# Another order for a routing stage and for the last units of an expert turn

## The chip, the core and the metric

The kernel runs on one core of a Trainium2 chip. TensorE (PE) multiplies matrices, VectorE (DVE) and ScalarE (ACT) work on tiles, GpSimd (POOL) and SyncE (SP) mostly issue transfers here. Each engine works through its own list of instructions in order and waits on semaphores for the others. The metric is the device time of one launch in microseconds (us).

## The reference, cut to what is computed

One step of a two-layer encoder over 256 prompt and 64 sample tokens (T = 320) of width 1024, all float32. Layer 0 is a pooling mixer and a dense SwiGLU, layer 1 is attention and then the part that matters here, eight experts of which each token takes two:

```
def _moe(h, w_router, b_router, w1, w3, w2):
    logits = jnp.einsum('btd,de->bte', h, w_router, ...) + b_router.astype(jnp.float32)
    vals, idx = lax.top_k(logits, TOP_K)
    gates = jax.nn.softmax(vals, axis=-1)
    gate_full = jnp.sum(jax.nn.one_hot(idx, N_EXPERTS, ...) * gates[..., None], axis=-2)
    y = jnp.zeros_like(h)
    for e in range(N_EXPERTS):
        y = y + gate_full[..., e:e + 1].astype(h.dtype) * _swiglu(h, w1[e], w3[e], w2[e])
    return y
...
        e_ple = p[i].astype(x.dtype) @ w_ple_proj[i]
        gate = jax.nn.sigmoid(_rmsnorm(x, g_ple[i]) @ w_ple_gate[i])
        x = x + gate * e_ple
```

The inner width of an expert is 3584.

## The kernel before

**Precision by three products.** Each operand is split in a high and a low part (`Sh`, `Sl` for weights, `Ah`, `Al` for activations), and a product is three matmuls: high by high, high by low, low by high. All matmuls of this kind pass the helper at line 609.

**Weights as units.** Weights come in units of 128 x 2048 numbers, 1 MB each. SP loads a unit into one of six slots of `raw` (line 207), ACT writes its high part into one of three slots of `Sh` in two halves (`hi`, line 365), DVE writes the low part into `Sl` in two halves (`lo`, line 961). SP may load unit q once the low part of unit q - 6 is done (line 206). ACT starts on unit q when PE is done with unit q - 3.

**Routing stage.** After the attention's output and a norm, PE multiplies by the router's weights, ACT adds the bias (line 555), PE transposes the logits (line 834). DVE takes the two largest of each token (lines 1172 to 1180), marks them in `sel` (line 1190), and builds the gates from an exponential that ACT computes (line 558). PE sums `sel` to give each token its place within its expert (`pos_done`), DVE turns this to `posm`, counts whether an expert has more than 128 tokens (lines 1204 to 1208, semaphore `routed`), builds one-hot rows for expert 0 (`one_hots`, line 1214), and PE makes from them the list of token numbers (`slot_info`), which DVE writes to `ix` (line 1226). Meanwhile the 320 token rows have to get to DRAM: PE transposes them in six blocks (`rows(0)` to `rows(5)`, line 827), ACT copies each block out of PSUM to `hrow` (line 564), SP stores three pieces to `rows_dram` (line 252). When all are stored, POOL issues an indirect DMA that gathers the 128 rows of expert 0 into `xrow` (line 341). PE transposes these (`gather`, line 851), ACT and DVE split them (lines 569 and 966), and the first expert unit can start. Before PE starts the loop, and before SP loads any unit beyond the first six of expert 0, each reads the count (`routed`).

**Expert turns.** A loop of m * 8 + 8 turns follows; here m is 0, so there are eight. A turn has 42 units n = 0 to 41: for each of seven blocks two units `g`, two units `u`, and behind the next block's two units `d`. The last eight units are g6 (34, 35), u6 (36, 37), d5 (38, 39) and d6 (40, 41). For each block, ACT takes the silu of g (line 587), DVE multiplies it with u (line 1264, semaphore `gum_ready`), PE transposes the product (`transposes`, line 900), ACT and DVE split it (`high_t`, line 581; `low_t`, line 966), and the two `d` units of that block multiply it. In the last units PE also transposes the next expert's rows (`gather(i + 2)`, line 851), which ACT and DVE split (`high_x`, `low_x`).

The order is written out by hand: each engine has its own program, with the actions of unit n ahead of its `hi(n + 3)` or `lo(n + 3)`. In the last units it is: before unit 38 the gather's transposes, between 38 and 39 `transposes(6)`, and d6 (unit 40) waits for `low_t(6)`. The lines that the change touches are 253, 557 to 564, 590 to 594, 824 to 845, 919 to 926, 1204 to 1232 and 1271 to 1275.

## Time and profile before

| | |
|---|---|
| median of 3 runs | 1625.07 us (1623.9 to 1625.52) |
| the profiled execution | 1625.96 us, of which the span from the first to the last instruction is 1623.9 us |
| mean granted TensorE clock | 0.977 of full speed |
| busy, share of the span | PE 1535.5 us (95%), DVE 1227.1 us (76%), ACT 1010.6 us (62%), POOL 43.9 us (3%) |
| routing stage | about 538 to 571 us of the span |
| the eight expert turns | about 571 to 1557 us, 123.3 us each |

The profile gives times in us from the span's start. A busy PE is no PE at its peak, since matmuls are pipelined: what counts is the step from one start to the next. In the turns the step of a matmul with 512 columns is 0.23 us.

### The profile page before, as it was taken

The numbers are of one execution on the slowest core, as the hardware profiler recorded it, in microseconds if no ns is written. First come the engines' busy times: TensorE is split into PE (matmuls) and PEld (weight loads), VectorE is DVE, ScalarE is ACT, GpSimd is POOL, SyncE is SP. The second block draws the span as 40 slices with busy tenths as digits, with TensorE's granted clock in tenths as the row PEclk, the third lists the DMA queues.
The fourth block names the chain that finished last, engine by engine and source line by source line (L and its number), as shares of the span: only waits on it lengthen the run. The fifth ranks groups of instructions, "written<-read, shape, count | busy, mean of one in ns | idle before, by whom it ended". The sixth has DMA issues, their size and how long they took to land.

```text
span 1623.9 us, 23510 instructions
## 1 busy us (share of the span) xinstructions
PE 1535.5 (95%) x8088; PEld 1333.8 (82%) x8088; DVE 1227.1 (76%) x1484; ACT 1010.6 (62%) x1289; POOL 43.9 (3%) x45
## 2 busy tenths in 40 slices
PE   2799999999899599999999999999999999999987
PEld 1699999999889388888878878878878888888877
DVE  6643434446754479999999999999899899899884
ACT  2433333345554367777777777777777777777763
POOL 6000000000000000000000000000000000000000
PEclk7999999999999789999999999999999999999999
DMA  7154444443320369989999989989989989999930
GB/s 277 30 175 140 151 155 155 140 154 130 116 86 27 120 229 373 379 333 375 370 339 374 379 331 372 384 334 369 379 333 373 381 338 363 375 340 357 383 121 33
DMA packets 64552, 429.33 MB, mean 264 GB/s; under 512 B 8208, under 2 KB 11920, under 8 KB 13440
## 3 DMA queue, kind: packets, MB, share of 16 engines
q1 hardware_dynamic: 61232, 423.24, 68.8%
q0 software_dynamic: 1392, 4.90, 0.9%
q10 hardware_dynamic: 1888, 0.64, 0.2%
q8 instruction: 26, 0.43, 0.1%
q14 instruction: 14, 0.11, 0.0%
HBM read 425.49 MB, written 3.27 MB: 264 GB/s over the span
## 4 chain that ended last, share of the span: by engine, by line
PE 86%; DVE 8%; issue 3%; ACT 2%; DMA 1%; SPq 0%; DVEq 0%; ACTq 0%; POOLq 0%
PE PS L609 84%; DVE s_Sl L961 2%; DVE s_Al L966 2%; PE PS L900 1%; DVE s_rstd L970 1%; ACT s_Sh L365 1%; DVE s_hT L983 1%; DMA s_G<-rows_dram,s_ix 1%; DMA s_raw<-in_w_trunk 1%; DVE s_G L1007 1%; PE PS L780 0%; DVE s_hT L1029 0%; DVE s_G L1022 0%; DVE s_hT L1027 0%; ACT s_std L382 0%
## 5 line engine op out<-in xcount | busy, mean ns | idle before, releaser
L961 DVE TENSOR_TENSOR s_Sl<-s_raw,s_Sh 128x1024 fp32r<-128x1024 f32 x790 | 929.9, 1220 | 205.9 <-ACT s_Sh L365 201.4
L365 ACT ACTIVATE s_Sh<-s_raw 128x1024 fp32r<-128x1024 f32 x798 | 800.2, 1053 | 272.6 <-PE PS L609 269.2
L609 PE MATMUL PS<-s_Sh,s_Ah 128*128 128x512 f32 x1344 | 531.9, 396 | 10.0 <-DVE s_Al L966 10.0
L609 PE MATMUL PS<-s_Sh,s_Al 128*128 128x512 f32 x1344 | 525.3, 391 | 0.0
L609 PE MATMUL PS<-s_Sl,s_Ah 128*128 128x512 f32 x1344 | 525.3, 391 | 0.0
L609 PE MATMUL PS<-s_Ah,s_Sh 128*128 128x320 f32 x1008 | 317.7, 315 | 41.1 <-DVE s_Al L966 39.9
L609 PE MATMUL PS<-s_Al,s_Sh 128*128 128x320 f32 x1008 | 315.0, 313 | 0.0
L609 PE MATMUL PS<-s_Ah,s_Sl 128*128 128x320 f32 x1008 | 315.0, 313 | 0.0
L609 PEld LDWEIGHTS PS<-s_Sh,s_Ah 128*128 128x128 f32 x1344 | 253.3, 188 | 62.5 <-DVE s_Sl L961 12.6
L609 PEld LDWEIGHTS PS<-s_Sh,s_Al 128*128 128x128 f32 x1344 | 253.0, 188 | 54.2
L609 PEld LDWEIGHTS PS<-s_Sl,s_Ah 128*128 128x128 f32 x1344 | 253.4, 189 | 48.5
L609 PEld LDWEIGHTS PS<-s_Ah,s_Sh 128*128 128x128 f32 x1008 | 192.5, 191 | 46.1 <-issue 37.6
L609 PEld LDWEIGHTS PS<-s_Al,s_Sh 128*128 128x128 f32 x1008 | 192.6, 191 | 0.2
L609 PEld LDWEIGHTS PS<-s_Ah,s_Sl 128*128 128x128 f32 x1008 | 192.4, 191 | 0.0
L966 DVE TENSOR_TENSOR s_Al<-PS,s_Ah 128x512 fp32r<-128x512 f32 (+1 forms) x82 | 53.7, 663 | 17.1 <-ACT s_Ah L569 11.5
L587 ACT ACTIVATE s_G<-PS 128x512 f32<-128x512 f32 x56 | 33.5, 599 | 43.1 <-PE PS L609 43.1
L388 ACT ACTIVATE s_Ah<-s_hT 128x320 fp32r<-128x320 f32 x48 | 22.1, 469 | 53.9 <-DVE s_hT L1029 27.4
L412 ACT ACTIVATE s_sq<-PS 128x320 f32<-128x320 f32 x28 | 10.7, 434 | 67.0 <-PE PS L609 67.0
L966 DVE TENSOR_TENSOR s_Al<-s_G,s_Ah 128x640 fp32r<-128x640 f32 x14 | 11.5, 825 | 41.5 <-ACT s_Ah L416 41.5
L416 ACT ACTIVATE s_Ah<-s_G 128x640 fp32r (+1 forms) x14 | 10.2, 736 | 52.3 <-PE PS L609 46.9
L1053 DVE TENSOR_TENSOR s_G<-s_sq,PS 128x320 f32 (+1 forms) x28 | 12.4, 484 | 39.5 <-PE PS L609 39.5
L609 PE MATMUL PS<-s_sq,s_ones 128*128 128x320 f32 x112 | 33.9, 459 | 7.5 <-POOL s_lg L308 5.9
(156 smaller groups left out, 771.4 us busy)
## 6 DMA issues: line engine op xcount, KB each, us to landing
s_raw<-in_w_moe SPq DMA_DIRECT2D x336, 1024.0 KB, 4.9
s_raw<-in_w_trunk SPq DMA_DIRECT2D x63, 1024.0 KB, 4.9
s_xT<-in_xT SPq DMA_DIRECT2D x2, 640.0 KB, 5.4
out_yT<-s_hT SPq DMA_DIRECT2D x4, 320.0 KB, 2.4
rows_dram<-s_G SPq DMA_DIRECT2D x2, 512.0 KB, 2.8
s_pT<-in_pT ACTq DMA_DIRECT2D x1, 320.0 KB, 24.2
s_pT<-in_pT SPq DMA_DIRECT2D x1, 320.0 KB, 3.1
rows_dram<-s_G SPq DMA_DIRECT2D x1, 256.0 KB, 3.1
```

The lines of the kernel that those rows point to most:

```text
L365: nc.scalar.activation(Sh[:, q % NSPL, o:o + UNIT // 2], raw[:, q % NRAW, o:o + UNIT // 2], ACT.Copy).then_inc(hi_ready, 1)
L388: nc.scalar.activation(Ah3[:, c, :], hT[:, c, :], ACT.Copy).then_inc(hh_ready, 1)
L412: nc.scalar.activation(sg[:, f, :], PS[:, f, 0:T], ACT.Silu).then_inc(silu_done, 1)
L587: nc.scalar.activation(sgm[:, b % 2, :], PS[:, 2 + 2 * (b % 2), :], ACT.Silu).then_inc(msilu_done, 1)
L609: return nc.tensor.matmul(out, w, m, start=start, stop=stop, **kw)
L900: last = nc.tensor.transpose(PS[:, 0, P * q:P * q + P], gum[:, b % 2, P * q:P * q + P], ident[:, :])
L961: last = nc.vector.tensor_tensor(Sl[:, q % NSPL, o:o + UNIT // 2], raw[:, q % NRAW, o:o + UNIT // 2], Sh[:, q % NSPL, o:o + UNIT // 2].bit ...
L966: return nc.vector.tensor_tensor(out, x, high.bitcast(F32), ALU.subtract).then_inc(done, 1)
L970: link(nc.vector.reciprocal(rstd[:, :], std[:, :]))
L983: nc.vector.scalar_tensor_tensor(out=hT[:, c, :], in0=xT[:, c, :], scalar=vec[:, g, c:c + 1], in1=rstd[:, :], op0=ALU.mult, op1=ALU.mult). ...
L1007: nc.vector.scalar_tensor_tensor(out=hcat[:, c, o:o + b - a], in0=xT[:, c, a:b], scalar=vec[:, G_MIX0, c:c + 1], in1=rstd[:, a:b], op0=ALU ...
L1053: nc.vector.tensor_tensor(out(f), sg[:, f, :], PS[:, 2 + f, 0:T], ALU.mult).then_inc(gu_ready, 1)
```

## The change

Nothing is computed in another way; instructions stand in another order, and one wait is added.

- ACT copies the row blocks 0, 1 and 2 ahead of the exponential of the gates and 3, 4 and 5 behind it, and loads the silu table behind all six. Before, all six stood behind the exponential and the table load.
- PE transposes all five remaining row blocks ahead of the sums over `sel`. Each block has a PSUM bank of its own (2 + n, before 2 + n % 4), so that blocks 4 and 5 wait for no copy.
- DVE builds the one-hot rows of expert 0 first and counts for `routed` afterwards.
- SP waits for the gathered rows (`xrow_loaded`) before it reads the count and goes on loading units 6, 7 and so on of expert 0.
- In the last units of a turn, `transposes(6)` with `high_t(6)` and `low_t(6)` stand directly behind the gather's transposes, ahead of unit 38 and ahead of `high_x` and `low_x`; before, they stood behind unit 38.

```diff
                 sp.dma_start(rows_dram[P * t:P * t + r, :], hrow[0:r, t, :]).then_inc(rows_stored, 16)
+            sp.wait_ge(xrow_loaded, 16)
             sp.wait_ge(routed, 1)
...
-            act.wait_ge(top_ready, 1)
-            nc.scalar.activation(rt[:, :, 1], rt[:, :, 0], ACT.Exp).then_inc(gexp_ready, 1)
-            table(ACT.Silu)
             for n in range(6):
+                if n == 3:
+                    act.wait_ge(top_ready, 1)
+                    nc.scalar.activation(rt[:, :, 1], rt[:, :, 0], ACT.Exp).then_inc(gexp_ready, 1)
                 act.wait_ge(hrow_done, n + 1)
                 t, half = n // 2, n % 2
                 r = TS if t == 2 else P
-                nc.scalar.activation(hrow[0:r, t, 512 * half:512 * half + 512], PS[0:r, 2 + n % 4, :], ACT.Copy).then_inc(hrow_ready, 1)
+                nc.scalar.activation(hrow[0:r, t, 512 * half:512 * half + 512], PS[0:r, 2 + n, :], ACT.Copy).then_inc(hrow_ready, 1)
+            table(ACT.Silu)
...
                     if n == NU - 4:
+                        high_t(NBK - 1)
                         high_x(0, i * 2 + 3)
                         high_x(1, i * 2 + 4)
-                    if n == NU - 3:
-                        high_t(NBK - 1)
...
-                if n >= 4:
-                    pe.wait_ge(hrow_ready, n - 3)
                 for q in range(4):
-                    last = nc.tensor.transpose(PS[0:r, 2 + n % 4, P * q:P * q + P], hT[:, 4 * half + q, P * t:P * t + r], ident[:, :])
+                    last = nc.tensor.transpose(PS[0:r, 2 + n, P * q:P * q + P], hT[:, 4 * half + q, P * t:P * t + r], ident[:, :])
...
-            rows(1)
-            rows(2)
+            for n in range(1, 6):
+                rows(n)
             pe.wait_ge(sel_ready, 1)
...
             last.then_inc(pos_done, 1)
-            for n in range(3, 6):
-                rows(n)
...
                         gather(i + 2)
+                        transposes(NBK - 1)
...
-                        if POS[kind, b] + h == NU - 3:
-                            transposes(NBK - 1)
...
             one_hots(0, 1)
+            link(most)
+            nc.vector.tensor_scalar(cnt[0:1, 1:2], cnt[0:1, 0:1], float(P), None, ALU.is_gt)
...
+            nc.vector.tensor_copy(extra[0:1, 0:1], cnt[0:1, 3:4]).then_inc(routed, 1)
             take_slots(1)
...
                     if n == NU - 4:
+                        low_t(NBK - 1)
                         low_x(0, i * 2 + 3)
                         low_x(1, i * 2 + 4)
-                    if n == NU - 3:
-                        low_t(NBK - 1)
```

How the instructions then stand, engine by engine (no time is in these rows; the changed kernel's line numbers differ by a few). First place, ACT in the routing stage: `s_G` is the tile that holds `hrow`, the 3-column `s_rt` is the exponential. Before:

```order
L555 ACTIVATE s_lgT<-PS,s_br 8x320 [waits lgT_done,small_loaded]
L558 ACTIVATE s_rt<-s_rt 128x3 [waits top_ready]
L372 ACT_TABLE_LOAD
L372 ACTIVATE s_spare<-s_eps 128x1
L564 ACTIVATE s_G<-PS 128x512 [waits hrow_done] x4
L564 ACTIVATE s_G<-PS 64x512 [waits hrow_done] x2
```

And now:

```order
L556 ACTIVATE s_lgT<-PS,s_br 8x320 [waits lgT_done,small_loaded]
L565 ACTIVATE s_G<-PS 128x512 [waits hrow_done] x3
L561 ACTIVATE s_rt<-s_rt 128x3 [waits top_ready]
L565 ACTIVATE s_G<-PS 128x512 [waits hrow_done]
L565 ACTIVATE s_G<-PS 64x512 [waits hrow_done] x2
L373 ACT_TABLE_LOAD
L373 ACTIVATE s_spare<-s_eps 128x1
```

Three copies moved ahead of the exponential, and the table load behind all six. Second place, SP between the row stores and the first load of the loop. Before:

```order
L252 DMA rows_dram<-s_G 128x1024 [waits hrow_ready] x2
L252 DMA rows_dram<-s_G 64x1024 [waits hrow_ready]
L254 TENSOR_LOAD s_extra [waits routed]
L254 ISA x2
L255 UNCONDITIONAL_BRANCH
L255 ISA
L207 ISA [waits lo_ready]
L207 DMA s_raw<-in_w_moe 128x2048
```

And now:

```order
L252 DMA rows_dram<-s_G 128x1024 [waits hrow_ready] x2
L252 DMA rows_dram<-s_G 64x1024 [waits hrow_ready]
L255 TENSOR_LOAD s_extra [waits routed,xrow_loaded]
L255 ISA x2
L256 UNCONDITIONAL_BRANCH
L256 ISA
L207 ISA [waits lo_ready]
L207 DMA s_raw<-in_w_moe 128x2048
```

The read of the count, and with it every later load, now also waits for the gathered rows. Third place, the last units of a turn, PE from the gather's transposes on. Before:

```order
L851 MATMUL PS<-s_ident,s_G 128x128 [waits xrow_loaded]
L851 MATMUL PS<-s_ident,s_G 128x128 x7
L619 REGISTER_ALU [waits tl_ready]
L609 MATMUL PS<-s_Sh,s_Ah 128x512 [waits lo_ready]
L609 MATMUL PS<-s_Sl,s_Ah 128x512
```

And now:

```order
L848 MATMUL PS<-s_ident,s_G 128x128 [waits xrow_loaded]
L848 MATMUL PS<-s_ident,s_G 128x128 x7
L894 REGISTER_ALU
L897 MATMUL PS<-s_ident,s_G 128x128 [waits tl_ready,gum_ready]
L897 MATMUL PS<-s_ident,s_G 128x128 x3
L620 REGISTER_ALU [waits tl_ready]
L610 MATMUL PS<-s_Sh,s_Ah 128x512 [waits lo_ready]
```

The four transposes of the last product, with their wait for it, stand ahead of unit 38's matmuls. On DVE at the same place (the 128x1024 rows are halves of weight passes, `th_ready` is the product's split, `xh_ready` that of the gathered rows), before:

```order
L961 TENSOR_TENSOR s_Sl<-s_raw,s_Sh 128x1024 [waits hi_ready]
L959 REGISTER_ALU
L961 TENSOR_TENSOR s_Sl<-s_raw,s_Sh 128x1024 [waits hi_ready]
L1220 ISA
L966 TENSOR_TENSOR s_Al<-PS,s_Ah 128x512 [waits xh_ready]
L1220 REGISTER_ALU
L966 TENSOR_TENSOR s_Al<-PS,s_Ah 128x512 [waits xh_ready]
L959 REGISTER_ALU
L961 TENSOR_TENSOR s_Sl<-s_raw,s_Sh 128x1024 [waits hi_ready]
L959 REGISTER_ALU
L961 TENSOR_TENSOR s_Sl<-s_raw,s_Sh 128x1024 [waits hi_ready]
L966 TENSOR_TENSOR s_Al<-PS,s_Ah 128x512 [waits th_ready]
```

And now:

```order
L1261 TENSOR_TENSOR s_G<-s_G,PS 128x512 [waits unit_done]
L955 REGISTER_ALU
L957 TENSOR_TENSOR s_Sl<-s_raw,s_Sh 128x1024 [waits hi_ready]
L955 REGISTER_ALU
L957 TENSOR_TENSOR s_Sl<-s_raw,s_Sh 128x1024 [waits hi_ready]
L962 TENSOR_TENSOR s_Al<-PS,s_Ah 128x512 [waits th_ready]
L1212 ISA
L962 TENSOR_TENSOR s_Al<-PS,s_Ah 128x512 [waits xh_ready]
L1212 REGISTER_ALU
L962 TENSOR_TENSOR s_Al<-PS,s_Ah 128x512 [waits xh_ready]
```

The split of the product moved ahead of the two of the gathered rows and of one weight pass; the product itself (first row, line 1264 before) keeps its place ahead of the weight pass of unit 40.

## Rows read from the trace of the kernel before

**Rows 1.** The page, section 4: what ended last, by engine.
```profile
PE 86%; DVE 8%; issue 3%; ACT 2%; DMA 1%; SPq 0%; DVEq 0%; ACTq 0%; POOLq 0%
```
**Rows 2.** PE's waits, whole span: us in total, times, longest.
```profile
PE PS L851 <- DMA s_G<-rows_dram,s_ix: 12.4, 1, 12.4
```
**Rows 3.** The chain, 540 to 575 us: start, us, what.
```profile
555.38 3.11 DMA rows_dram<-s_G
...
559.39 8.81 DMA s_G<-rows_dram,s_ix
...
568.24 1.13 PE PS L851 x4
...
570.96 4.21 PE PS L609 x9
```
**Rows 4.** Timeline of ACT, 546 to 557: start, us, operation, idle before.
```profile
550.69 0.21 ACT L558 ACTIVATE s_rt<-s_rt 128x3 f32<-128x3 f32 x1 [1.84 <-DVE s_rt L1180]
...
552.32 3.03 ACT L564 ACTIVATE s_G<-PS 128x512 f32<-128x512 f32 x6
```
**Rows 5.** Timeline of PE, 546 to 572 us.
```profile
549.16 1.09 PE L827 MATMUL PS<-s_ident,s_hT 128*128 128x128 f32 x8
551.54 0.18 PE L609 MATMUL PS<-s_sel,s_trib 128*128 128x8 bf16 x1 [1.29 <-DVE s_sel L1190]
```
**Rows 6.** Timeline of DVE, 548 to 572 us.
```profile
551.40 0.16 DVE L1193 TENSOR_SCALAR s_rt<-s_rt 128x3 f32<-128x3 f32 x1
...
552.53 0.18 DVE L1201 SCALAR_TENSOR_TENSOR s_posm<-PS,s_sel 128x24 f32<-128x24 f32 x1
...
555.91 0.15 DVE L1226 CAST s_ix<-PS 128x1 uint32<-128x1 f32 x1
```
**Rows 7.** Timeline of SP's queue, 480 to 640 us.
```profile
553.41 2.43 SPq L252 DMA_DIRECT2D rows_dram<-s_G  x3
558.25 81.12 SPq L207 DMA_DIRECT2D s_raw<-in_w_moe  x24
```
**Rows 8.** Gather, line 341: nine issues, times to landing.
```profile
L341 POOL DMA_INDIRECT s_G<-rows_dram,s_ix x9: 1049/1160/1183, 559.4 to 1515.2; - x9
...
DMA to landing us min/median/max: 5.1/5.6/8.9
```
**Rows 9.** DMA queues, 559.3 to 563.8 us: packets, MB, share of engines.
```profile
q1 hardware_dynamic: 213, 1.61, 91.4%
```
**Rows 10.** The same from 559.3 to 568.3 us.
```profile
q0 software_dynamic: 144, 0.52, 15.6%
```
**Rows 11.** The same from 652.3 to 655.4 us, the second gather.
```profile
q1 hardware_dynamic: 129, 0.97, 75.1%
q0 software_dynamic: 15, 0.06, 4.8%
```
**Rows 12.** The page, section 6: an expert load, KB, us to landing.
```profile
s_raw<-in_w_moe SPq DMA_DIRECT2D x336, 1024.0 KB, 4.9
```
**Rows 13.** Stretches: us, busy share of engines, PEclk, DMA share, GB/s.
```profile
61.65:65.04 3.39, 3.39 (x13) 3.39 (x14) 3.39 (x9) 1.86 (x4) 0.00 (x0) 0.50 0.02 5
...
570.96:577.04 6.08, 6.08 (x14) 4.84 (x15) 1.41 (x3) 1.07 (x2) 0.00 (x0) 0.50 0.00 0
```
**Rows 14.** Timeline of PE, end of turn 2, 806.4 to 815.3.
```profile
806.71 1.03 PE L851 MATMUL PS<-s_ident,s_G 128*128 128x128 f32 x8
807.50 0.47 PE L609 MATMUL PS<-s_Sh,s_Ah 128*128 128x512 f32 x1
...
813.31 0.39 PE L609 MATMUL PS<-s_Sh,s_Al 128*128 128x512 f32 x1
814.86 0.49 PE L609 MATMUL PS<-s_Sh,s_Ah 128*128 128x512 f32 x1 [1.16 <-DVE s_Al L966]
```
**Rows 15.** Timeline of DVE, the same stretch.
```profile
805.45 2.35 DVE L961 TENSOR_TENSOR s_Sl<-s_raw,s_Sh 128x1024 fp32r<-128x1024 f32 x2
807.71 0.68 DVE L1264 TENSOR_TENSOR s_G<-s_G,PS 128x512 f32<-128x512 f32 x1
...
814.05 0.68 DVE L966 TENSOR_TENSOR s_Al<-PS,s_Ah 128x512 fp32r<-128x512 f32 x1
```
**Rows 16.** Waits of all engines, 700 to 1550 us: total, times, longest.
```profile
ACT s_Sh L365 <- PE PS L609: 164.7, 228, 2.2
...
PE PS L609 <- DVE s_Al L966: 7.0, 6, 1.2
```

More of the change, by code:

```diff
@@ L1203, in _ @@
             nc.vector.tensor_scalar(posm[:, :, :], posm[:, :, :], -1.0, None, ALU.add).then_inc(stepped, 1)
-            link(nc.vector.reduce_max(cnt[0:1, 0:1], PS[0:1, 1, 24:32], AX.X))
-            nc.vector.tensor_scalar(cnt[0:1, 1:2], cnt[0:1, 0:1], float(P), None, ALU.is_gt)
-            link(nc.vector.tensor_scalar(cnt[0:1, 2:3], cnt[0:1, 0:1], float(2 * P), None, ALU.is_gt))
-            link(nc.vector.tensor_tensor(cnt[0:1, 3:4], cnt[0:1, 1:2], cnt[0:1, 2:3], ALU.add))
-            nc.vector.tensor_copy(extra[0:1, 0:1], cnt[0:1, 3:4]).then_inc(routed, 1)
+            most = nc.vector.reduce_max(cnt[0:1, 0:1], PS[0:1, 1, 24:32], AX.X)
             def one_hots(e, steps):
@@ L1232, in _ @@
             one_hots(0, 1)
+            link(most)
+            nc.vector.tensor_scalar(cnt[0:1, 1:2], cnt[0:1, 0:1], float(P), None, ALU.is_gt)
+            link(nc.vector.tensor_scalar(cnt[0:1, 2:3], cnt[0:1, 0:1], float(2 * P), None, ALU.is_gt))
+            link(nc.vector.tensor_tensor(cnt[0:1, 3:4], cnt[0:1, 1:2], cnt[0:1, 2:3], ALU.add))
+            nc.vector.tensor_copy(extra[0:1, 0:1], cnt[0:1, 3:4]).then_inc(routed, 1)
             take_slots(1)
```

## The prediction

> **What bounds the kernel.** I read the chain of what ended last, then PE's waits, then the two places that the diff touches, engine by engine in order of time. PE carries 86% of the chain [rows 1], so time can go only where PE stands still or where its work shrinks, and the change shrinks none. Two standstills lie where it works. The large one is a single wait of 12.4 us for the gathered rows of expert 0 [rows 2]. The chain shows what it is made of [rows 3]: the last store of token rows is issued at 555.38 and takes 3.11 us; POOL issues the gather at 559.39, 0.90 us after that landing; the gather takes 8.81 us, to 568.20; and 2.76 us of transposes and splits follow until the first expert matmul at 570.96. The small one comes once a turn: unit 40's first matmul starts 1.55 us after unit 39's last, where the step is 0.23, so 1.32 us are lost to the split of the last product [rows 14, 15]; the waits count it six times for six turns, 1.2 us at most [rows 16], and it is alike in all eight.
>
> **Routing, first half: the stores start earlier.** The six copies run at 0.505 us each, from 552.32 to 555.35, behind the exponential at 550.69 and a table load [rows 4]. The blocks they copy are ready sooner than that. PE did blocks 1 and 2 in 1.09 us from 549.16, 0.55 us a block [rows 5]; with five blocks in a row, block 5 is done at about 551.9 to 552.0. So three copies fit ahead of the exponential, which slips from 550.69 to about 550.9, and the other three run from about 551.1 to 552.6. The last store is then issued near 552.65 and not at 555.38: **2.7 us earlier**. What hides the slips: the exponential's result is first used at 551.40 [rows 6], 0.3 us after it would be there. The sums over `sel` start at 551.54 [rows 5] and move behind block 5, to about 551.95; their 0.4 us end at about 552.4, just before DVE needs them at 552.53 [rows 6]. Without that cover the list of token numbers would be later by what it slips, but that list is ready at 556.06 [rows 6] and POOL's new issue would be at 552.65 + 3.11 + 0.90 = 556.66, so another 0.6 us are free even if DVE's count, now behind the one-hot rows, brought nothing. The table load and the weight pass behind the copies fall into PE's wait and cost nothing. Ends for this term: 2.3 if the copies run into the blocks or the exponential, 3.0 if they don't at all.
>
> **Routing, second half: the gather alone.** Before, SP issues loads from 558.25 on [rows 7], ahead of the gather. In the first 4.4 us after the gather's issue every one of the 213 packets belongs to those loads [rows 9]; then its 144 packets go beside them, 15.6% of 9.0 us or 1.4 us of engine time in all [rows 10]. Now SP waits until the gather has landed, so nothing runs beside it. No row shows a gather alone. From above: the late start may be the gather's own, since it is the kernel's first, and then it takes 4.4 + 1.4 + some 0.4 to finish, 6.2 us. From below: the second gather has its first 15 packets within 3.1 us although loads take 75% of the engines [rows 11]; 2.8 + 1.4 gives 4.2 us. I take 5.6 us, the median of the nine gathers [rows 8]: same instruction, same bytes, and between the two ends. That gives 8.8 - 5.6 = **3.2 us** (2.6 to 4.6).
>
> The Trainium skill (DMA: Bandwidth & Descriptors, Queues, rings and completion order) says that each DMA engine takes turns between the queues that have work for it, packet by packet, which speaks against the wait on SP: loads would slow a gather but not hold it back. The packets after 563.8 agree [rows 10], the empty 4.4 us don't follow from it [rows 9]. By that rule the late start is the gather's own and the term is 8.8 - 6.2 = 2.6 us. The skill (SBUF — State Buffer, Who interferes with whom) also has a DVE instruction with two SBUF inputs hold up a GpSimd instruction that reads SBUF; the gather would now be issued beside DVE's weight pass. The trace shows 1.05 us for the first issue and 1.18 at most with DVE busy [rows 8], a cost of 0.1; by the page one whole DVE half pass, 1.2 us, could be lost, and the sum would be 1618.0.
>
> **What the new wait holds up.** Behind it in SP's queue stand the reading of the count and every load from unit 6 on. The gather now lands at about 556.66 + 5.6 = 562.3. From the end of the last store's issue at 555.84 to the first load SP took 2.4 us [rows 7], with `routed` set long before; so the first load goes at 564.7, lands 4.9 us later [rows 12] at 569.6, and the next two at steps of some 2.6. PE starts expert 0 near 565.0 and the first six units are in place. A unit is twelve matmuls: about 5.1 us at the half clock, then 3.0. ACT wants unit 6 when unit 3 is done, near 579. So the loads have some 9 us to spare, and this wait costs nothing; in the turns before, ACT never waited for a load [rows 16].
>
> **The clock.** PE restarts at the half clock, 0.50, and kept it for 6.08 us from 570.96 on; elsewhere it kept it for 3.39 us after a pause [rows 13]. A matmul's step is 0.425 there against 0.23, so each us of it costs 0.46. It may thus bring up to 1.2 us, or cost some 0.3. I count zero.
>
> **The end of a turn.** Now `transposes(6)` stand right behind the gather's, ahead of unit 38. They need the product, and DVE makes that from 807.71 to 808.39, since the weight pass that began at 805.45 is in front of it [rows 15]; nothing there is moved. PE would be free at 807.50 [rows 14]. A release takes 0.13 us (814.05 + 0.68 to 814.86), so PE stands from 807.50 to 808.52: 1.02 us. What came late is then early: split by ACT at 809.8, by DVE behind its pass at 811.3, and d6 wants it at 814.6. So a wait of 1.32 us is replaced by one of 1.02: 0.30 us a turn, eight turns, **2.4 us**. Queued behind on ACT and DVE are the split of the next rows, not needed before the next turn, and the passes for unit 41, which would be done near 815.3 and are wanted near 817.3. Ends: 0 if the restart behind the transposes costs again what it costs today, 3.6 if DVE is a little earlier.
>
> **The sum.** 2.7 + 3.2 + 2.4 = 8.3 us. Against the profiled execution, 1625.96, that is 1617.7; that run is 0.9 above the median, and from the median, 1625.07, it is **1616.8 us**. All low ends with 0.3 for the clock: 2.3 + 2.6 + 0 - 0.3 = 4.6, so 1620.5. All high ends with 1.2: 3.0 + 4.6 + 3.6 + 1.2 = 12.4, so 1612.7. A measurement of this kernel can tell about 0.2%, 3.25 us, from no change.
>
> **Rivals.**
> - The gather is slow on its own account: without loads it still takes 6.2 to 8.8 us. For it speaks the empty start [rows 9], against it the eight later ones [rows 8]. At 8.8 the term is gone: 1625.07 - 5.1 = 1620.0; at 6.2 it is 1617.4. By the skill's rule on taking turns, above, this is the case. Chance 0.12.
> - All terms near their high ends: about 1613. Chance 0.10.
> - The wait at the turn's end goes altogether, as the order suggests if the product were ready: 8 x 1.32 = 10.6 in place of 2.4, so 1608.5. DVE's rows speak against it [rows 15]. Chance 0.04.
> - The weights come late: PE stops at unit 6 and gives the gain back. It decides from a first load that lands 9 us later than worked out, after 579; some 8 us beyond that is no change, 1625. Against it stand the spare time and the six loaded units. Chance 0.04.
> - **Slower:** PE's new wait for the product is longer than the old one. If DVE came to the product only after the next weight pass, 2.35 us [rows 15], the wait would be 3.4 us in place of 1.32, 8 x 2.05 = 16.4 us, and with 5.9 gained in routing the time 1635.6. It is slower by over 0.2% from a wait of 1.32 + (5.9 + 3.25) / 8 = 2.5 us a turn. The order of DVE's rows speaks against it: the product stays ahead of that pass. Chance 0.04.
>
> **Chances.** The forecast, 1614.5 to 1619, has 0.66. Faster by over 0.2% are the forecast, the slow gather, the high ends and the vanished wait: 0.92; within 0.2% 0.04; slower 0.04. From 1613.0 to 1620.5 lie the forecast, the slow gather and most of the high ends, about 0.86; the others are left out.
>
> **What would show it.** In the changed profile the last row store should be issued near 552.6 and the gather near 556.7; it should land in 4.2 to 6.2 us, and SP's next load should come only after it; the first expert matmul near 565. ACT should show no wait for a load of expert weights. At each turn's end PE's wait for the split of the last product should be gone, and one of about 1.0 us for the product should stand ahead of unit 38. I am wrong if the gather still takes over 8 us, if PE waits at unit 6 for weights, or if the new wait is over 1.3 us.

## The result and the profile after

The changed kernel takes 1615.23 us (median of four runs, 1614.95 to 1615.46) against 1625.30 (1623.9 to 1625.55) measured beside it: a ratio of 0.994 with a 95% interval of 0.9922 to 0.9957, 10.1 us less. The forecast was 1616.8 us with a range of 1613.0 to 1620.5, 8.3 us less. The profiled execution took 1615.06 us, its span 1613.0 us, 10.9 less than the span before.

**Where the time went.** I cut both spans at three points that both traces have: the start of the reciprocal of the norm ahead of the router (539.19 before), the first expert matmul (570.96 before), and the first transpose of the gathered rows in turn 8.

| stretch | before | after | difference |
|---|---|---|---|
| start to the norm's reciprocal | 539.19 | 538.26 | -0.93 |
| reciprocal to the first expert matmul | 31.77 | 24.57 | -7.20 |
| from there to the last transposes of gathered rows | 975.37 | 970.37 | -5.00 |
| from there to the end | 77.58 | 79.81 | +2.23 |

The chain of what ended last, by engine (the page of the changed kernel; answers to [rows 1]):

```profile
PE 89%; DVE 6%; issue 2%; ACT 2%; DMA 1%; SPq 0%; DVEq 0%; ACTq 0%; POOLq 0%
```

The chain of the routing stage, 540 to 575 us of the changed kernel: start, us, what (answers to [rows 3]):

```profile
551.19 3.09 DMA rows_dram<-s_G
...
555.18 4.89 DMA s_G<-rows_dram,s_ix
...
560.11 1.13 PE PS L848 x4
...
562.83 12.30 PE PS L610 x44
```

From the norm's reciprocal on, the last store is issued after 12.93 us and not after 16.19. 0.36 of these 3.26 us lie in the router's matmuls, whose clock differs between the two executions; 2.9 are the change's. The gather takes 4.89 us in place of 8.81, 3.92 less. PE's waits, whole span: us in total, times, longest (answers to [rows 2, 16]):

```profile
PE PS L848 <- DMA s_G<-rows_dram,s_ix: 6.8, 1, 6.8
PE PS L897 <- DVE s_G L1261: 5.7, 8, 0.7
```

The long wait fell from 12.4 to 6.8 us. The second row is the new wait for the product, once in each turn. PE's old wait for the split, `DVE s_Al`, has no row any more between 700 and 1550 us, and ACT and PE have none for a load of expert weights. ACT in the routing stage (timeline; start, us, operation, idle before; answers to [rows 4]):

```profile
547.57 0.60 ACT L565 ACTIVATE s_G<-PS 128x512 f32<-128x512 f32 x1
548.56 1.09 ACT L565 ACTIVATE s_G<-PS 128x512 f32<-128x512 f32 x2 [0.39 <-PE PS L826]
549.53 0.21 ACT L561 ACTIVATE s_rt<-s_rt 128x3 f32<-128x3 f32 x1
549.63 1.54 ACT L565 ACTIVATE s_G<-PS 128x512 f32<-128x512 f32 x3
551.19 1.28 ACT L373 ACT_TABLE_LOAD   x1
```

Three copies stand ahead of the exponential, which starts 0.1 us after its input is there, and the other three follow without a gap. The gathers (line 342; answers to [rows 8]) and the DMA queues from 555.1 to 560.1 us (answers to [rows 9, 10]):

```profile
L342 POOL DMA_INDIRECT s_G<-rows_dram,s_ix x9: 1157/1162/1760, 555.2 to 1502.1; - x9
...
DMA to landing us min/median/max: 4.9/5.8/7.8
```
```profile
q0 software_dynamic: 144, 0.52, 31.7%
```

The gather's 144 packets are alone, since no other queue has a row. By the packets' own times the first comes 2.47 us after the issue; before it was 4.50. POOL's instruction, though, takes 1.76 us, where it took 1.05 before: the maximum in the first row is this gather. SP's queue (answers to [rows 7]):

```profile
549.18 2.47 SPq L252 DMA_DIRECT2D rows_dram<-s_G  x3
561.41 77.90 SPq L207 DMA_DIRECT2D s_raw<-in_w_moe  x27
```

The first load goes 1.34 us after the rows have landed (555.18 + 4.89 = 560.07). Turn 2's end, PE and then DVE (answers to [rows 14, 15]):

```profile
797.41 1.03 PE L848 MATMUL PS<-s_ident,s_G 128*128 128x128 f32 x8
799.16 0.66 PE L897 MATMUL PS<-s_ident,s_G 128*128 128x128 f32 x4 [0.71 <-DVE s_G L1261]
799.57 0.47 PE L610 MATMUL PS<-s_Sh,s_Ah 128*128 128x512 f32 x1
799.88 0.39 PE L610 MATMUL PS<-s_Sl,s_Ah 128*128 128x512 f32 x1
...
804.89 0.39 PE L610 MATMUL PS<-s_Sh,s_Al 128*128 128x512 f32 x1
805.12 0.39 PE L610 MATMUL PS<-s_Sh,s_Ah 128*128 128x512 f32 x1
```
```profile
796.15 2.35 DVE L957 TENSOR_TENSOR s_Sl<-s_raw,s_Sh 128x1024 fp32r<-128x1024 f32 x2
798.42 0.68 DVE L1261 TENSOR_TENSOR s_G<-s_G,PS 128x512 f32<-128x512 f32 x1
799.02 2.35 DVE L957 TENSOR_TENSOR s_Sl<-s_raw,s_Sh 128x1024 fp32r<-128x1024 f32 x2
801.29 1.88 DVE L962 TENSOR_TENSOR s_Al<-PS,s_Ah 128x512 fp32r<-128x512 f32 x3
```

Eight transposes took 0.79 us before (806.71 to 807.50 in [rows 14]), so PE could have gone on at 798.20; the product's transposes start at 799.16, 0.96 us later and 0.06 after the product is done. Counted by steps it is a little less: from the eighth transpose to the ninth it takes 0.98 us, where one transpose follows the other by 0.11, so PE stands 0.87 us. Unit 40 follows unit 39 at 805.12 at the plain step of 0.23. The turn went from 123.27 to 122.63 us: 0.64 less, eight times 5.1.

**The clock.** Of the remaining differences none lies where the change is. Half-clock stretches (PEclk 0.50, the level of 1.2 GHz) fall at other places in the two executions. Ahead of the norm, the one near 410 us lasts 6.83 us in the kernel before and 3.41 in the changed one, which comes to it 0.3 us late and leaves it 0.9 us early. Behind the restart of the experts they got shorter, 6.08 to 4.93 us ([rows 13] and the first row here); behind turn 8 they got longer, which the last row of each kernel shows (columns as in [rows 13]; first the changed kernel, then the kernel before):

```profile
562.83:567.76 4.93, 4.93 (x12) 3.87 (x13) 1.41 (x3) 0.52 (x1) 0.00 (x0) 0.50 0.95 394
...
1554.22:1561.05 6.83, 6.25 (x14) 4.00 (x13) 1.00 (x3) 1.59 (x4) 0.00 (x0) 0.50 0.00 0
```
```profile
1580.56:1583.97 3.41, 3.25 (x12) 2.90 (x12) 3.24 (x8) 3.20 (x9) 0.00 (x0) 0.50 0.00 0
```

What the longer one covers stands in PE's rows: the sixteen sums of squares of the norm behind the last turn, which follow each other by 0.53 us at the half clock and by 0.27 otherwise (timeline; first the changed kernel, then the kernel before):

```profile
1555.78 7.17 PE L610 MATMUL PS<-s_sq,s_ones 128*128 128x320 f32 x16 [0.58 <-DVE s_xT L1242]
```
```profile
1569.18 4.57 PE L609 MATMUL PS<-s_sq,s_ones 128*128 128x320 f32 x16 [0.59 <-DVE s_xT L1245]
```

Of the 14 kernels profiled here, six have 6.83 us of it there: these sums take 6.9 to 7.2 us, and the last stretch lasts 79.0 to 79.8. The other eight have 3.41 us behind these sums or none (but for one at the very end, which all 14 have): the sums take 4.57 us, and the last stretch lasts 76.0 to 77.6, a shorter end of turn 8 included. So some 2.8 us of any kernel here hang on where that stretch falls. In this execution the clock gave -0.93 ahead of the norm, -0.36 at the router, -0.55 behind the restart and +2.87 at the end (the 2.23 of the table and the 0.64 that turn 8 saves there), +1.0 in all. The change itself is worth 2.9 + 3.9 + 5.1 = 11.9 us, of which 10.9 are seen.

### The profile page after: what moved, and what is told of

Same layout as the page of the kernel before. It is cut to its first block, busy times and chain, and to the rows that moved or that the text cites. A ratio compares the mean times of both kernels' runs of the same rounds, so it can differ in the third digit from the quotient of the medians.

```text
span 1613.0 us, 23511 instructions
## 1 busy us (share of the span) xinstructions
PE 1535.2 (95%) x8088; PEld 1334.2 (83%) x8088; DVE 1227.6 (76%) x1484; ACT 1012.1 (63%) x1289; POOL 44.6 (3%) x45
## 4 chain that ended last, share of the span: by engine, by line
PE 89%; DVE 6%; issue 2%; ACT 2%; DMA 1%; SPq 0%; DVEq 0%; ACTq 0%; POOLq 0%
PE PS L610 87%; PE PS L897 1%; DVE s_rstd L966 1%; DVE s_Al L962 1%; DVE s_Sl L957 1%; DVE s_hT L979 1%; ACT s_Sh L366 1%; DMA s_raw<-in_w_trunk 1%; DVE s_G L1003 1%; DVE s_hT L1025 0%; PE PS L781 0%; DVE s_G L1018 0%; DVE s_G L1261 0%; DVE s_hT L1023 0%; DMA s_G<-rows_dram,s_ix 0%
## 5 line engine op out<-in xcount | busy, mean ns | idle before, releaser
L1049 DVE TENSOR_TENSOR s_G<-s_sq,PS 128x320 f32 (+1 forms) x28 | 12.4, 484 | 39.5 <-PE PS L610 39.5
```

What stands on the lines that cost most here:

```text
L1049: nc.vector.tensor_tensor(out(f), sg[:, f, :], PS[:, 2 + f, 0:T], ALU.mult).then_inc(gu_ready, 1)
```

## The experiments

Each kernel was timed beside the kernel before on the same chip. "Norm to experts" is the stretch from the norm's reciprocal to the first expert matmul, "turn" the distance of the gathered rows' transposes from turn to turn, both from the profiled execution.

| kernel | norm to experts | turn | median, us | ratio to before (95%) |
|---|---|---|---|---|
| before | 31.77 | 123.27 | 1625.30 | |
| changed | 24.57 | 122.63 | 1615.23 | 0.9940 (0.9922 to 0.9957) |
| turn's end alone | 31.85 | 122.67 | 1622.18 | 0.9983 (0.9974 to 0.9992) |
| routing alone | 25.03 | 123.27 | 1617.99 | 0.9959 (0.9946 to 0.9973) |
| changed, without SP's wait | 29.19 | 122.67 | 1617.17 | 0.9956 (0.9942 to 0.9969) |
| SP's wait alone | 27.10 | 123.27 | 1619.96 | 0.9971 (0.9960 to 0.9982) |
| loads behind POOL's begin | 29.79 | 122.63 | 1618.11 | 0.9951 (0.9934 to 0.9967) |
| one load let through | 26.64 | 122.63 | 1615.48 | 0.9936 (0.9920 to 0.9953) |
| weight pass behind | 24.17 | 122.67 | 1612.35 | 0.9918 (0.9901 to 0.9934) |
| loads after unit 0 | 24.86 | 122.67 | 1616.61 | 0.9944 (0.9928 to 0.9961) |
| loads after unit 4 | 24.83 | 122.65 | 1626.26 | 1.0006 (0.9996 to 1.0015) |
| product between the halves | 24.59 | 121.87 | 1609.15 | 0.9900 (0.9883 to 0.9916) |
| split first | 24.86 | 121.80 | 1608.45 | 0.9891 (0.9875 to 0.9908) |
| split first and pass behind | 23.73 | 121.80 | 1605.97 | 0.9881 (0.9865 to 0.9898) |

### The parts of the change, one by one

The turn's end alone (the last hunks of the three engines in the diff above, nothing else):

> The kernel before with the new order of the last units of a turn alone; the routing stage is as before. Theory (the turn's gain is the smaller wait plus one restart of PE less): a turn takes 122.63 us as in the changed kernel and not 123.27, 8 x 0.64 = 5.1 us, so about 1620.2 us. Rival (the turn brings what the prediction gave it, 0.30 a turn, and the rest of the gain lies in routing): 1622.9 us, a turn of 122.97. In both the gather keeps its 8.8 us and its first data 4.4 us after the issue.

Everything but that:

> The changed kernel with the old order of the last units of a turn; routing is all new. Theory: from the norm's reciprocal to the first expert matmul 24.6 us and not 31.8, so 7.2 us less, of which the clock in the router's matmuls may be 0.4; turns of 123.27 us; about 1618.1 to 1618.5 us. Rival (routing brings the predicted 5.9): 1619.4 us.

The whole change without the one line of SP:

> The changed kernel without SP's wait for the gathered rows, so that loads of expert weights are again issued about when the gather is. Theory (the loads hold the gather back): the gather takes 7 to 8.8 us in place of 4.9, its first data come over 4 us after the issue, and the time is 2.1 to 3.9 us above the changed kernel, 1617.3 to 1619.1. Rival (the late start was the first gather's own, or came of its later moment): the gather stays at 4.9 to 5.8 us and the time at 1615.2 to 1616.1.

That line alone, put into the kernel before:

```diff
+            sp.wait_ge(xrow_loaded, 16)
             sp.wait_ge(routed, 1)
```

> The kernel before with SP's wait alone. Theory: the gather takes 4.9 us and not 8.8, nothing else moves, 3.9 us less: 1621.4 us. Rival (the gather's late start is its own): 8.8 us stay less the 1.4 to 2 us of sharing, and the time is 1623.3 to 1625.3. A rival on the other side: loads that start later make PE wait at unit 6, slower than 1625.3.

Norm to experts adds up: SP's wait alone brings 4.67 us, the routing's order without it 2.58, together 7.25, and the changed kernel has 7.20. So does the turn: 0.60 to 0.64 us with the turn's end, nothing without. The parts of the routing's order on ACT, PE and DVE have no run each. DVE's can have given little: the list of token numbers is done at 553.58 in the changed kernel, 0.7 us ahead of the last store's landing, and the count that moved behind it takes some 0.5 us. The median of the turn's end alone agrees less well with its trace. Its span is 4.8 us shorter than before, its eleven runs reach from 1620.47 to 1623.5, and the mean granted clock goes down from 0.979 to 0.973 as the time goes up. The trace decides there for the larger gain a turn, the median lies between the two. Routing alone and the change without SP's wait lie within 0.2 us of the lower ends that the theory gave them. SP's wait alone gained more than expected, since its gather took 4.13 us. The changed kernel's, with the same wait, took 4.89, and without the wait the gather was worse than before, 9.58. In order: SP's wait alone, the change without it (chains of the routing stage):

```profile
559.62 4.13 DMA s_G<-rows_dram,s_ix
```
```profile
554.91 9.58 DMA s_G<-rows_dram,s_ix
```

### Why the gather starts late beside loads

SP lets the loads go as POOL begins the first gather's issue, in place of when it has landed:

```diff
-            sp.wait_ge(xrow_loaded, 16)
+            sp.wait_ge(fetch_begun, 1)
```

> The changed kernel with SP waiting only until GpSimd begins the first gather's issue, not until the rows have landed: the weight loads then stand behind the gather in time and share its transfer. Theory (the first gather was late because up to three loads had been put in the queues ahead of it; sharing alone is mild, as in the seven later turns, 5.1 to 6): its first packet 2.4 to 2.9 us after the issue, its landing after 5.0 to 6.5 us in place of 4.9, so 1615.3 to 1616.9. Rival (any load at the same time holds the gather back): 8 to 9.6 us as in the two kernels without the wait, 1618.3 to 1620.

The rival held: 9.79 us, a little over its 8 to 9.6 (the median, 1618.11, is a little under its 1618.3). The issue begins at 556.20 and takes POOL 1.81 us, and three loads follow it within 1.89 us. SP's queue, the gather in the chain, and the DMA queues from 556.2 to 561.4 and from 561.5 to 564.5:

```profile
556.71 1.71 SPq L207 DMA_DIRECT2D s_raw<-in_w_moe  x3
```
```profile
556.20 9.79 DMA s_G<-rows_dram,s_ix
```
```profile
q1 hardware_dynamic: 175, 1.30, 68.5%
```
```profile
q1 hardware_dynamic: 95, 0.75, 61.0%
q0 software_dynamic: 105, 0.43, 35.0%
```

For 5.2 us there is no packet of the gather, then the two queues go on side by side, packet for packet. So holding the loads back until the gather's begin is not enough. The next kernel lets exactly one load through at that moment:

```diff
+            sp.wait_ge(fetch_begun, 1)
...
                     expert(i % NE, n, i * RND)
+                    if n == NRAW:
+                        sp.wait_ge(xrow_loaded, 16)
```

> The changed kernel with exactly one weight load let through as GpSimd begins the first gather's issue, and the others only once the rows have landed. Before this run: no load near it, first packet after 1.7 to 2.5 us; one load issued 1.3 us ahead of it, as in each later turn, 2.4 to 2.9 us; three loads around it 4.5 to 5.3 us, also where they were issued 0.5 to 1.9 us behind its begin. Theory (the gather gets no packet until the loads that were issued before GpSimd's instruction ended have drained, and later loads share one for one): the one load is issued 0.5 us after the begin and drains by 4.3 to 4.9 us, where the gather's first packets come; alone from there it lands after 6.2 to 6.9 us: 1616.5 to 1617.5. Rival (a gather beside one load simply takes turns with it): first packet at 2.4 to 2.9 us, landing after 5.0 to 5.7: 1615.3 to 1616.1.

The theory held in the trace. One load of 1.05 MB, 0.5 us behind the begin, holds the gather's first packet back to 4.59 us, and 0.98 MB of it have passed by then; after that the gather is nearly alone and lands after 6.61. From 556.2 to 560.7, and from 556.2 to 562.8 us:

```profile
q1 hardware_dynamic: 120, 0.98, 64.5%
```
```profile
q1 hardware_dynamic: 144, 1.05, 46.4%
q0 software_dynamic: 144, 0.52, 19.4%
```

The time doesn't tell the two apart: the median, 1615.48, lies in the rival's range, but the four runs fall in two pairs, near 1613.4 and 1617.5, and the profiled one, 1617.43, is of the upper. Norm to experts is 2.1 us longer. The theory also explains most of the turns, which the prediction had used as its lower bound: there the load on its way, issued 1.3 us ahead of the gather, is nearly through 2.8 us after the issue, just when the gather's packets start, and the next is issued 1.7 us behind. These gathers look as if they shared, and mostly they run in a gap. A few don't fit: the changed kernel's sixth gather has its first packet after 2.88 us, though the load ahead of it lands only after 5.52, and four gathers of the kernel with the product between the halves start after 2.9 to 3.0 beside a load that lands after 5.8 to 6.7. They too are late, landing after 7.8 to 9.8 us, but to say that no packet comes before the earlier loads are through is too strict. What the runs don't settle is why three loads hold it back for 1.3 to 1.7 MB only and not for all three, that is, whether the order of issue or some depth decides.

The Trainium skill (DMA: Bandwidth & Descriptors, Queues, rings and completion order) has each DMA engine take turns between its queues. The rows agree for the time from the gather's first packet on. For the time ahead of it, 4.5 to 5.3 us beside three loads and 1.7 to 2.5 beside none, they don't, unless the gather's queue has nothing to send yet, which no row shows.

### Why the gather alone took 4.9 us and not 4.1

DVE's weight pass of unit 2 of expert 0 ran beside POOL's issue. Here it stands behind the split of the gathered rows:

```diff
-            lo(Q_O + 6)
             low_x(0, 1)
...
+            lo(Q_O + 6)
```

> The changed kernel with the weight pass of unit 2 of expert 0 on VectorE moved from ahead of the split of the first gathered rows to behind it, so that VectorE stands still while GpSimd issues the first gather. Theory (that pass, with two SBUF inputs, draws out the issue: 1.76 to 1.81 us where the pass ran beside it, 1.05 where it didn't, as in the kernel with SP's wait alone): the issue takes 1.05 us again, the gather 4.1 to 4.3 in place of 4.9, and the first expert matmul comes 0.6 to 0.8 us sooner after the norm: 1614.3 to 1614.8, if the moved pass is in time for unit 2, which wants it some 4 us later. Rival (the longer issue comes from the earlier stores or from the empty queue): the issue stays at 1.7 to 1.8 us, and the time at 1615.2. Second rival: TensorE waits at unit 2 for the pass, 1616 or more.

POOL's issue, first of the changed kernel, then of this one, and this one's gather in the chain:

```profile
555.18 1.76 POOL L342 DMA_INDIRECT s_G<-rows_dram,s_ix  x1 [19.93 <-DMA rows_dram<-s_G]
```
```profile
556.46 1.05 POOL L342 DMA_INDIRECT s_G<-rows_dram,s_ix  x1 [20.27 <-DMA rows_dram<-s_G]
```
```profile
556.46 4.14 DMA s_G<-rows_dram,s_ix
```

The pass costs the first gather 0.75 us, as the theory said. Norm to experts falls by 0.40 only, since the changed kernel's router matmuls had the 0.36 of the clock that this kernel's hadn't. The time fell by more, 2.9 us, because the last stretch lasts 76.97 us here: some 2.1 of it are the clock's. The Trainium skill (SBUF — State Buffer, Who interferes with whom) says that a DVE instruction with two SBUF inputs holds up a GpSimd instruction that reads SBUF; the first issue agrees, with 0.71 us. The eight issues in the turns don't: they take 1.15 to 1.18 us while the same passes run beside them. What differs there stays open.

### How much time the loads had

SP waits also for the end of TensorE's first expert unit (`Q_MOE + 1`), and in the second kernel for that of the fifth (`Q_MOE + 5`):

```diff
             sp.wait_ge(xrow_loaded, 16)
+            sp.wait_ge(unit_done, Q_MOE + 1)
```

> The changed kernel with SP waiting also for the end of TensorE's first expert unit, at about 567.9, before it loads unit 6 and the following ones: the first load some 7 us later than in the changed kernel, landing near 574. Theory (the loads have spare time: ScalarE wants unit 6 at 577.3 and waits for TensorE, not for loads): no change, 1614.5 to 1616, and no wait of ScalarE or TensorE for an expert load. Rival (the time that the loads lose is missing later in the first turn): ScalarE waits for loads in the first turn and the time is 1616.5 to 1622.

> The changed kernel with SP waiting for the end of the fifth expert unit, near 580, before it loads unit 6: the load lands near 586, some 9 us after ScalarE wants it. This measures from where on late loads cost. Theory (ScalarE's and VectorE's passes need 3.8 us from the landing, and TensorE wants the unit at 583.5): TensorE stands 5.5 to 6.5 us at unit 6, with up to 1.5 us more for a restart at the half clock: 1620.5 to 1623. Rival (later units make part of it good, since loads step at 2.6 us and units at 3.0): 1617.5 to 1620. No change at all, 1615.2, would mean that unit 6 is wanted much later than the trace is read here.

Loads that start some 8 us later, counted from the first expert matmul, leave no wait of ACT or PE for an expert load; norm to experts is within 0.3 us of the changed kernel's and the turn within 0.04. The median, 1616.61, is 0.6 us over what the theory gave and just inside the rival's range. Nothing in the trace ties that to the loads: the reciprocal alone, ahead of all of them, comes 1.0 us later than in the changed kernel, at 539.27. In the second kernel the first load goes at 583.20 and lands at 588.04. ACT's and PE's rows of it, and the half-clock stretch:

```profile
588.14 2.00 ACT L367 ACTIVATE s_Sh<-s_raw 128x1024 fp32r<-128x1024 f32 x2 [10.38 <-DMA s_raw<-in_w_moe]
```
```profile
592.05 0.63 PE L611 MATMUL PS<-s_PT,s_Ah 128*128 128x320 f32 x1 [8.20 <-DVE s_xT L1243]
```
```profile
586.50:596.75 10.25, 4.70 (x14) 3.92 (x15) 6.33 (x7) 6.49 (x8) 0.00 (x0) 0.50 1.01 427
```

ACT is 10.4 us late, PE 8.2, and the 4.70 us that PE works at the half clock add 2.2 (0.46 for each): 10.4, where the first turn is 10.8 longer. PE's row names an addition on DVE, which stands behind the split of unit 6 there. My expectation, 5.5 to 6.5 and 1.5 and a time of 1620.5 to 1623, was too low: I had taken the landing two us too early, and the half clock only for the restart's first matmuls.

### What is left at the turn's end

DVE makes the product of unit 37 between the two halves of the weight pass in front of it (`product` is the three lines that stood ahead of the pass of unit 40):

```diff
                 for half in range(2):
+                    if half and between:
+                        between()
                     v.wait_ge(hi_ready, r * (2 * NRAW) + (2 * q + half + 1))
...
-                    lo(Q_MOE + n + NSPL, i * RND)
+                    lo(Q_MOE + n + NSPL, i * RND, (lambda: product(n + 1, b)) if n == NU - 6 else None)
```

> The changed kernel with one thing more: in the last units of a turn VectorE makes the product of unit 37 between the two halves of the weight pass of unit 39 and not behind both. Theory (the 0.87 us that TensorE still stands ahead of unit 38 are the product's, which is late by the second half of that pass, 1.2 us): the product is ready at some 0.9 us behind the first gathered-row transpose, when those transposes end, so the wait goes to 0 to 0.1 us and nothing else becomes late, since the half pass that now comes 0.7 us later is wanted some 3 us later. The turn falls from 122.63 to some 121.75 us, eight times 0.8 to 0.95: 1607.5 to 1609. Rival (another wait stands behind it, the weights of unit 39 or the split wanted by unit 40): the wait moves and the turn stays within 0.2 us of 122.63, 1613.5 to 1615.5.

PE's and DVE's rows at the end of turn 2:

```profile
797.92 1.03 PE L848 MATMUL PS<-s_ident,s_G 128*128 128x128 f32 x8
798.86 0.66 PE L897 MATMUL PS<-s_ident,s_G 128*128 128x128 f32 x4
```
```profile
796.66 1.22 DVE L959 TENSOR_TENSOR s_Sl<-s_raw,s_Sh 128x1024 fp32r<-128x1024 f32 x1
798.12 0.69 DVE L1263 TENSOR_TENSOR s_G<-s_G,PS 128x512 f32<-128x512 f32 x1 [0.24 <-PE PS L610]
798.72 3.49 DVE L959 TENSOR_TENSOR s_Sl<-s_raw,s_Sh 128x1024 fp32r<-128x1024 f32 x3
```

The product now waits for unit 37 itself, and PE for 0.07 us (0.18 from the eighth transpose to the ninth, 0.11 without a wait). The turn is 0.76 shorter, and the median, 1609.15, lies just above the range that the theory gave. The other way leaves the transposes where they were and moves only the split:

```diff
                     if n == NU - 4:
-                        low_t(NBK - 1)
                         low_x(0, i * 2 + 3)
                         low_x(1, i * 2 + 4)
+                        low_t(NBK - 1)
```

`high_t` in the same way, and `transposes(NBK - 1)` ahead of unit 39 again.

> The changed kernel with the last product's transposes back behind unit 38, where they stood before, but with its split on ScalarE and VectorE directly behind that of the gathered rows, ahead of the weight passes of unit 41. Theory (the old wait of 1.32 us ahead of unit 40 was made by the place of the split behind VectorE's weight pass of 2.36 us, not by the place of the transposes): the split is ready some 1 us ahead of unit 40 and the product was wanted only behind unit 38, so no wait is left at all: a turn of some 121.7 to 121.9 us, 1607 to 1609. Rival (moving the transposes was what took the old wait away): the wait ahead of unit 40 is back at 0.9 to 1.5 us and the turn at 122.6 to 123.3, 1615 to 1620.

```profile
801.50 0.60 PE L897 MATMUL PS<-s_ident,s_G 128*128 128x128 f32 x4
801.86 0.48 PE L610 MATMUL PS<-s_Sh,s_Ah 128*128 128x512 f32 x1
```
```profile
798.89 0.68 DVE L1262 TENSOR_TENSOR s_G<-s_G,PS 128x512 f32<-128x512 f32 x1
799.49 2.35 DVE L958 TENSOR_TENSOR s_Sl<-s_raw,s_Sh 128x1024 fp32r<-128x1024 f32 x2
801.76 1.88 DVE L963 TENSOR_TENSOR s_Al<-PS,s_Ah 128x512 fp32r<-128x512 f32 x3
```

PE, then DVE: the product is late as ever, but nobody wants it before 801.50, and its split comes in the group of three at 801.76, ahead of the next pass. PE has no wait left between 680 and 1520 us, and the turn is 121.80, 0.83 shorter than in the changed kernel and 1.47 shorter than before. So the old wait was made by the split's place behind the pass; that the transposes moved was not needed.

Both gains in one kernel, this one and the weight pass behind:

> The changed kernel with two edits that each gained alone: the last product's split directly behind that of the gathered rows with its transposes back behind unit 38 (turn of 121.80 in place of 122.63 us), and the weight pass of unit 2 of expert 0 behind the split of the first gathered rows (gather 4.14 in place of 4.89 us). Theory (they lie in different stages and add): 1615.2 - 8 x 0.83 - 0.75 = 1607.8; with the shorter stretch at the half clock after the restart that the second edit had alone, down to 1605.5. Rival (the gain of the second was only another phase of the clock): 1608.5.

1605.97 us (1605.16 to 1606.66): it beats the changed kernel by 9 us and the kernel before by 1.2%. Its gather takes 4.10 us and its turn 121.80. Of these 9 us some 3 are the clock's in the last stretch, while the start lost 1.2 (reciprocal at 539.46).

## Why the prediction was right, step by step

**Stores, forecast 2.7, measured 2.9.** Right in size and reason: five blocks in a row, three copies ahead of the exponential, which slips by 0.1. Routing alone, with the same clock as before at the router, issues its last store 13.29 us after the reciprocal against 16.19.

**Gather, forecast 3.2, measured 3.9.** The mechanism holds, the size is the sum of two misses. I took 5.6 us from the median of the nine; a gather alone takes 4.1 (SP's wait alone, weight pass behind), my lower end. And I gave the weight pass beside the issue 0.1 us by the turns' rows, where it costs 0.75. 4.14 + 0.75 = 4.89. The rival that the late start is the first gather's own (0.12) is refuted: without loads it starts after 1.7 to 2.5 us.

**SP's wait costs nothing.** Right, with more room than worked out. The first load went at 561.41 and not at 564.7, since the gather ended 2.2 us sooner and SP needed 1.34 us and not 2.4. ACT wanted unit 6 at 577.3, 11 us after it lands at about 566.3. The rival of the late weights has its price measured: I had no change some 8 us beyond a landing at 579, and a landing at 588.04, 9 us beyond, gave a ratio of 1.0006.

**The turn's end, forecast 2.4, measured 5.1.** This is the term that was mis-sized, above its own high end of 3.6, though the wait it rests on is right: 1.02 was forecast, 0.96 came, for 1.32 before. What was wrong is the comparison of the two. The 1.32 is what goes beyond a plain step. The 1.02 is counted from 807.50, where the first matmul behind the transposes starts, only 0.03 us behind the last of them; a further transpose would start 0.11 behind it. By steps the new wait is 0.87, and the difference 0.45 a turn and not 0.30. More lies next to the waits: behind the old one PE's next step is 0.33 us for 0.23, behind the new one 0.16 for 0.11, and the transposes now stand in one group and not in two. From the first transpose of the gathered rows to the first matmul of the next turn PE takes 13.71 to 13.74 us before and 13.14 to 13.16 now, 0.6 less. The last 0.05 of the 0.64 is spread over steps elsewhere in the turn that no single row shows. I had named the restart as a possible cost, for the low end; it was a small gain. The two kernels of the last section show that a further 0.8 us a turn was open, which I had given to nobody.

**The clock, forecast zero, between -1.2 and +0.3.** It cost 1.0 in the profiled execution. I had looked only at the restart, where it did gain 0.55; the larger part came at the end, behind the last thing that the change touches. That the time lies in the forecast's 1614.5 to 1619 is in part luck: the change is worth 11.9 us and not 8.3, and without the clock's 1.0 the time would have been near 1614.2, still between 1613.0 and 1620.5.

**The rivals.** The longer wait of PE and the vanished wait didn't come. "All high ends" comes near to what the change is worth, 3.0 + 4.6 + 3.6 = 11.2 against 11.9, but not by its parts: the gather wasn't at its high end of 4.6, the turn lay beyond its own for another reason, and the clock cost time where this rival let it give 1.2.

## What to carry to other kernels

Before a long wait for a small transfer, look at what else was issued around it: holding back the bulk loads behind it was worth more than making its inputs earlier, and it cost nothing as long as the held loads landed before their first user asked for them. Where an engine waits for a small step that stands behind a big one on another engine, move the step that is wanted next, and look for the place where it is wanted last: moving the split alone was worth more than moving the whole group. Count an engine's time by the steps from start to start over the whole stretch, not by its waits alone: two waits that are counted from different moments don't compare.

## What the runs showed of the hardware

- A gather issued by POOL is held back by loads that are issued shortly before it or 0.5 us after its begin: 1.7 to 2.5 us to the first packet with none, 4.6 with one load 0.5 us behind, 4.5 to 5.3 with three, and beside three it shares packet for packet from its first packet on. In the turns, with loads on their way, the first packet comes after 2.4 to 3.3 us, in a few of them up to 3.7 us before the load ahead has landed.
- The first gather's issue takes 1.76 to 1.81 us beside a DVE weight pass and 1.05 without; in the turns 1.15 to 1.18 beside such passes.
- After a pause or a group of transposes the first step between two matmuls of 512 columns is 0.31 to 0.33 us and not 0.23. Behind transposes that costs nothing, since the first of the two starts 0.03 us behind the last transpose, where the step between transposes is 0.11.
- A stretch at the half clock of 6.83 us over the norm behind the last turn appears in six of the 14 profiled kernels and moves the time by some 2.8 us. Smaller gains than that had to be read from the stages, not from the medians.
